# Low parts of weight slots subtracted in four operations on GpSimd, and one slot of each layer's first MLP stage rounded in quarters

## The reference

```
for layer in range(2):
    if layer == 0:
        proj = h @ w_in_ab                                # 1024 -> 2048
        mix = concat(s5(u), stick_breaking(q, k, v)) @ w_out_ab
    else:
        q, f, i, g = split(h @ w_in_c, 4)                 # 1024 -> 4096
        mix = hgrn2(q, f, i, g) @ w_out_c
    h = layer_norm(alpha * h + mix)
    hid = square(relu(h @ w_up[layer] + b_up))            # 1024 -> 4096
    h = layer_norm(alpha * h + hid @ w_down[layer] + b_down)
```

## Time and profile before

| | before |
|---|---|
| median of 3 runs | 1326.92 us (1325.14 to 1329.05) |
| the profiled execution: its own time, its span | 1324.8 us, 1323.1 us |
| PE busy | 1278.1 us, 97% of the span |
| DVE busy | 812.9 us, 61% |
| ACT busy | 639.2 us, 48% |
| POOL busy | 329.7 us, 25% |
| mean granted clock of PE | 0.994 |

### The profile page before, as it was taken

The page is one execution under the profiler, slowest core; times in us unless marked ns, Lnnn a source line. Parts: engine busy times, 40 slices in busy tenths (PEclk is TensorE's granted clock), DMA queues, the critical chain, the costliest instruction groups (busy, mean ns, idle before and its releaser), DMA issues.

```text
span 1323.1 us, 23105 instructions
## 1 busy us (share of the span) xinstructions
PE 1278.1 (97%) x9734; PEld 1167.5 (88%) x9734; DVE 812.9 (61%) x1358; ACT 639.2 (48%) x992; POOL 329.7 (25%) x183
## 2 busy tenths in 40 slices
PE   7999999999999999999999999999999999999996
PEld 6999866989999999999888988877888898988984
DVE  6989664566577374574656366374666673745745
ACT  4344597455356254263554434454453472552634
POOL 0001172364200201103653224124651102010040
PEclk9999999999999999999999999999999999999997
DMA  6641100223223232222231112212222233233311
GB/s 192 150 102 34 66 1 1 97 65 96 96 85 108 97 96 96 96 97 96 64 96 64 62 51 77 69 63 69 92 79 81 96 120 99 92 105 96 104 56 64
DMA packets 112153, 111.50 MB, mean 84 GB/s; under 512 B 8145, under 2 KB 109729, under 8 KB 112049
## 3 DMA queue, kind: packets, MB, share of 16 engines
q1 hardware_dynamic: 108528, 106.77, 25.0%
q0 software_dynamic: 3120, 3.15, 1.5%
q10 hardware_dynamic: 400, 0.11, 0.0%
HBM read 107.91 MB, written 2.10 MB: 83 GB/s over the span
## 4 chain that ended last, share of the span: by engine, by line
PE 79%; DVE 10%; ACT 6%; issue 2%; POOL 1%; DMA 1%; DVEq 0%; SPq 0%; ACTq 0%
PE pb L858 42%; PE pb L1072 6%; PE pb L1074 6%; PE pb L1073 6%; PE pb L1033 2%; PE pb L1034 2%; PE pb L1035 2%; PE pb L870 1%; DVE sg L2695 1%; PE pb L969 1%; PE pb L968 1%; PE pb L1314 1%; PE pb L970 1%; ACT wh L1555 1%; DVE wl L2235 1%
## 5 line engine op out<-in xcount | busy, mean ns | idle before, releaser
L693 POOL TENSOR_TENSOR wl<-raw,wh 128x2048 fp32r<-128x2048 f32 x40 | 186.3, 4657 | 696.7 <-ACT wh L1555 696.7
L858 PE MATMUL pb<-hidl,wh 128*128 128x264 f32 (+1 forms) x744 | 197.4, 320 | 0.0
L858 PE MATMUL pb<-hidh,wh 128*128 128x264 f32 (+1 forms) x744 | 197.3, 319 | 0.0
L858 PE MATMUL pb<-hidh,wl 128*128 128x264 f32 (+1 forms) x744 | 197.2, 319 | 0.0
L1555 ACT ACTIVATE wh<-raw 128x2048 fp32r<-128x2048 f32 x72 | 137.4, 1908 | 93.4 <-DMA raw<-in_mlp_w_down 61.2
L858 PE MATMUL pb<-hh,wh 128*128 128x264 f32 (+1 forms) x584 | 150.9, 320 | 5.0 <-POOL wl L693 2.3
L858 PE MATMUL pb<-hh,wl 128*128 128x264 f32 (+1 forms) x584 | 145.7, 311 | 0.0
L858 PE MATMUL pb<-hl,wh 128*128 128x264 f32 (+1 forms) x584 | 145.4, 310 | 0.0
L858 PEld LDWEIGHTS pb<-hidh,wh 128*128 128x128 f32 x744 | 123.7, 188 | 9.6
L858 PEld LDWEIGHTS pb<-hidh,wl 128*128 128x128 f32 x744 | 123.4, 188 | 9.6
L858 PEld LDWEIGHTS pb<-hidl,wh 128*128 128x128 f32 x744 | 123.4, 188 | 9.6
(11 more groups left out here) (481 smaller groups left out, 3257.1 us busy)
## 6 DMA issues: line engine op xcount, KB each, us to landing
raw<-in_mlp_w_up SPq DMA_DIRECT2D x32, 1024.0 KB, 5.3
raw<-in_mlp_w_down SPq DMA_DIRECT2D x32, 1024.0 KB, 5.1
raw<-in_w_in_c SPq DMA_DIRECT2D x16, 1024.0 KB, 5.3
raw<-in_w_in_ab SPq DMA_DIRECT2D x8, 1024.0 KB, 7.0
raw<-in_w_out_ab SPq DMA_DIRECT2D x4, 1024.0 KB, 5.0
raw<-in_w_out_c SPq DMA_DIRECT2D x4, 1024.0 KB, 5.0
wl<-in_w_in_ab POOLq DMA_DIRECT2D x3, 1024.0 KB, 11.7
x_tok<-in_x SPq DMA_DIRECT2D x2, 1024.0 KB, 7.9
```

The source lines that it names most:

```text
L693: pool.tensor_tensor(wl[:, c % RING, :], raw[:, c % RING, :], wh[:, c % RING, :].bitcast(F32), ALU.subtract).then_inc(w_lo, 1)
L858: mm = pe.matmul(pb[:, bank + b, 0:z_ - a], lhs, rhs[:, a:z_], start=first and hi and k == 0, stop=last and k == len(todo) - 1)
```

## The change

The subtraction of a slot on POOL becomes four subtractions of 512 columns each. Each counts `w_lo` up by one, so PE waits for four per slot; the three slots in pieces add four at once. For slots 16 and 68 (`EARLY_HIGH`) ACT too makes the high part in four copies of 512 columns, and POOL waits for each quarter alone (`hi_quarter` for the first three, `w_hi` for the last). What is computed stays the same.

```diff
+EARLY_HIGH = [STAGES[f"up{layer}0"][0] + 3 for layer in range(2)]
...
             def low(c):
 
                 if c in LOWS_POOL:
-                    pool.wait_ge(w_hi, rank(c) + 1)
+                    if c not in EARLY_HIGH:
+                        pool.wait_ge(w_hi, rank(c) + 1)
                     if c in V16:
                         pool.wait_ge(v16_done, V16.index(c) + 1)
-                    pool.tensor_tensor(wl[:, c % RING, :], raw[:, c % RING, :],
-                                       wh[:, c % RING, :].bitcast(F32), ALU.subtract).then_inc(w_lo, 1)
+                    for k in range(4):
+                        q = slice(k * SLOT // 4, (k + 1) * SLOT // 4)
+                        if c in EARLY_HIGH and k < 3:
+                            pool.wait_ge(hi_quarter, 3 * EARLY_HIGH.index(c) + k + 1)
+                        elif c in EARLY_HIGH:
+                            pool.wait_ge(w_hi, rank(c) + 1)
+                        pool.tensor_tensor(wl[:, c % RING, q], raw[:, c % RING, q], wh[:, c % RING, q].bitcast(F32),
+                                           ALU.subtract).then_inc(w_lo, 1)
...
-                    pool.sem_inc(w_lo, 1)
+                    pool.sem_inc(w_lo, 4)
...
-                    pe.wait_ge(w_lo, LOWS_POOL.index(c) + 1)
+                    pe.wait_ge(w_lo, 4 * LOWS_POOL.index(c) + 4)
...
             def high(c):
 
-                if c < NSLOTS:
+                if c in EARLY_HIGH:
+                    act.wait_ge(w_in[c % RING], 16 * (c // RING + 1))
+                    for k in range(4):
+                        q = slice(k * SLOT // 4, (k + 1) * SLOT // 4)
+                        act.activation(wh[:, c % RING, q], raw[:, c % RING, q], ACT.Copy).then_inc(hi_quarter if k < 3 else w_hi, 1)
+                elif c < NSLOTS:
                     act.wait_ge(w_in[c % RING], 16 * (c // RING + 1))
                     act.activation(wh[:, c % RING, :], raw[:, c % RING, :], ACT.Copy).then_inc(w_hi, 1)
```

More of the change, by code:

```diff
@@ L404, in trunk @@
         w_lo = sem("w_lo")
+        hi_quarter = sem("hi_quarter")
         w_lo_dve = sem("w_lo_dve")
```

## The result

| | before | after |
|---|---|---|
| median of 12 runs | 1327.03 us (1324.52 to 1329.05) | 1329.76 us (1327.64 to 1331.99) |
| ratio after to before | | 1.003, 95% interval 1.0022 to 1.0037 |
| profiled execution, its time and span | 1324.8, 1323.1 us | 1331.22, 1329.4 us |
| mean granted clock of the profiled execution | 0.994 | 0.989 |

The change makes the kernel slower by 2.9 to 4.9 us by the ratio's interval; the medians lie 2.7 us apart, the means 3.4 us. The forecast was 1328.9 us in a range from 1323.4 to 1332.3.

The account below looks back on a forecast made before the run. PE, busy 97% of the span, was taken as the bound, so only its waits or slower matmuls count. Terms 0.80 + 0.44 + 0.87 + 0.9 + 0.7 - 3.3 + 1.6 = +2.0 us gave 1328.9 us; range 1323.4 to 1332.3.

Parts of the forecast that it names:

- Turns alternate: Likeliest case: POOL quarters and DVE instructions with two SBUF operands take turns; +2.0 us, 1328.9 us, chance 0.52.
- The rival in which queued quarters run through: POOL keeps DVE out until the slot is done; +1.2 us, 1328.1 us, chance 0.18.
- The rival in which the early quarters come first without DVE's turns: At slots 16 and 68 quarters precede DVE; pair-stage waits go; -3.9 us, up to -4.9, 1322.5 us, chance 0.13.
- A quarter's price: On POOL, four quarters in a row take 5.05 us against 4.61, so 0.44 us more a slot.
- Slot 68: Three DVE instructions between the quarters use up the early release; PE waits 0.80 us longer, 3.1 us.
- Slot 16: Three DVE instructions of 0.70 us come between the quarters; PE waits, +0.44 us.
- The layer norms: Norms 0, 1 and 2: later quarters hold up DVE, so PE waits longer; +0.87, +0.9 and +0.7 us.
- The pair stages: DVE gets in between quarters, so PE's waits for `qd` at three places go; -3.3 us together.
- The fourth place: A further `qd` wait of 1.7 us, ahead of the second pair; costed at 0, bound -1.0 us.
- The clock: One more stretch of PE at half clock behind the lengthened waits; +1.6 us, bounds -1.6 and +4.8.
- The rival of a slow clock behind the norms: Each lengthened wait is followed by half clock, three more stretches; +5.2 us, 1332.1 us, chance 0.17.

Follow-up runs that it names:

- Holding DVE back: Slots 16 and 68 alone in quarters, DVE waiting with the next stage's sums until POOL finished the slot, against the kernel before: 1324.7 us, ratio 0.9986.
- the two second profiles: One more profiled execution each of the kernel before (1325.59 us) and of the full change (1329.06 us), with nothing altered.

## Why the prediction was right or wrong

*The number* came out right in part by luck. The waits were forecast well in the main; the clock was forecast from one execution that was faster than most, and the sum was then carried over to the median, which already held more half clock than that execution. Forecast 1328.9 us, measured 1329.76 us.

*Turns alternate.* Right, and shown: in the changed kernel DVE and POOL alternate at slot 68, at slot 16, in the pairs and in norm 2. Holding DVE back (5.65 us) against letting it in (7.42 us) shows that the turns, and not the quarters, make slot 68 late. The rival in which queued quarters run through would have needed 5.05 us there. The rival in which the early quarters come first without DVE's turns wanted them done 5.2 us after ACT's start at slot 68 (989.4 against 984.16); they were done after 8.1 to 9.2 us.

*A quarter's price*, 0.44 us a slot by the spacing. Right: the four quarters of slot 13 in the changed kernel, with no DVE instruction that excludes them, take 5.04 us. The recorded spans, four of 1.30 us, would have said 5.20.

*Slot 68*, forecast +0.80 us, PE's wait 3.1 us, the last quarter 8.25 us after ACT's start. Two of three traces have 3.2 us and 8.1 or 8.2 us. The profiled execution had 4.51 us and 9.2 us; there the order of the first turn fell out the other way by 0.03 us, and the DMA of the slot took 7.1 us in place of 6.6. The step had taken the time of asking as fixed.

*Slot 16*, forecast +0.44 us: +0.64 us in the profiled execution, with a wait of 0.54 us, and a wait of 0.53 us with the two slots alone. A little undersized.

*The layer norms*, forecast +0.87, +0.9 and +0.7: measured +0.85, +0.85 and +0.66 us. Right in mechanism and size; with the norms' slots alone in quarters the `hh` waits grow by the same 2.2 us.

*The pair stages*, forecast -3.3: measured -3.5 us at these places in the change and alone. The fourth place was costed at nothing and its wait is 1.7 us as before.

*The clock*, forecast +1.6 us, is the mis-sized term. I read its state from one execution of the kernel before, in which one of four waits of 2 us and more was followed by half clock. That was a rare one: its mean clock was 0.994, which three of 53 timed executions of the same kernel reached, and their mean was 0.991. Over its 12 runs the changed kernel had 0.9885, so 0.0029 less; at half clock that is 0.0029 x 1330 x 2 = 7.7 us more, and as half of it is lost, up to 3.9 us and not 1.6. The terms without the clock sum to +0.4 us by the forecast; between the two second profiles the same places give 0.79 + 0.60 + 0.84 + 0.85 + 0.56 - 3.51 = +0.13 us, and their two further stretches (norm 0 and ahead of `out_c`) 1.5 and 1.6 us of the 3.4 us that lie between the ends. So the price of one stretch, 1.6 us, was about right (1.1 to 1.6 us for a first one), and their number was not: the forecast had one more, and it was two to four more. It is the clock that makes the kernel measurably slower, and the table of the twelve traces shows that the longer waits bring most of it: at the three norms 13 of 15 waits are followed by half clock instead of 7 of 21, which is 1.6 stretches more in an execution, where the 7.7 us above are a little over two. The stretch ahead of `out_c` comes behind a wait that did not change, so not all of a trace's count is the change's doing. The forecast's "nowhere else inside the span" also overlooks the last 13 us, at half clock in both kernels, which changes nothing between them.

*The rival of a slow clock behind the norms* (+5.2 us) had the right mechanism, and by its own sign, three more stretches, it comes nearer than the likeliest case: the profiled execution had four more than the first profile of before (1331.22 us), the second profile three more (1329.06 us). But norm 1 stayed without one in both, and as the kernel before has more than one stretch in most executions, the medians moved by 2.7 us and not by 5.2.

## What to carry to other kernels

Cutting a long POOL instruction was worth it here where DVE has a short chain with two SBUF operands that is caught behind it: there, three cut slots gave 3.3 us, and forty gave a loss. Where POOL itself is on the path, pieces let DVE in between, and the end comes later though the start came earlier; give such work to DVE (3.5 us here), or keep DVE away for as long (2.0 us). Before a clock term is taken from one trace, look at the mean granted clock of all runs, since one execution can be the lucky one.

## What the runs showed of the hardware

- POOL and DVE take turns of one instruction each: with both engines queued, each got one, even when POOL's next was already issued without a wait of its own. At slot 68 four quarters that take 5.04 us when nothing comes between took 8.47 us with three DVE instructions of 1.2 us between them, 7.42 us with one of 0.7 and two of 1.2 us, and 5.65 us with the one of 0.7 us.
- A DVE copy of 128x9 elements is held as well: in the changed kernel L2876 (`elast<-qd`) took 1.24 us beside a quarter, in place of 0.16 us.
- Half clock came behind waits of PE of 1.8 us too (4 of 12 traces), in some executions of a program and not in others. Two such stretches came one after the other behind 4.5 us, behind 3.2 us (slots 16 and 68 alone) and behind 2.8 us (the norms' slots alone). A stretch cost 1.1 to 1.6 us, a second one 0.7 us.
